# Decay exponents with their mask in one product per head, and large tiles that begin at multiples of 128 bytes

## The reference

```python
acs = jnp.cumsum(dt_k * a_g, axis=1)
seg = acs[:, :, None] - acs[:, None, :]
lmat = jnp.exp(jnp.where(causal, seg, -jnp.inf))
cb = jnp.einsum("blgn,bsgn->blsg", c_k, b_k)
w = cb[..., None] * lmat * dt_k[:, None]
y = jnp.einsum("blsgh,bsghp->blghp", w, x_k)
```

## Time and profile before

| | us |
|---|---|
| median of 3 runs | 1204.3 |
| their lowest and highest | 1203.85 and 1208.6 |
| the profiled execution | 1204.32 |
| its span | 1202.5 |

### The profile page before, as it was taken

One profiled execution on the slowest core, in us unless ns is written; L12 is line 12 of the kernel. 1 busy time (PEld: TensorE's weight loads), 2 busy tenths in 40 slices (PEclk: granted clock), 3 DMA queues, 4 the chain that ended last, 5 costly groups with the idle time before them and its releaser, 6 DMA issues.

```text
span 1202.5 us, 23183 instructions
## 1 busy us (share of the span) xinstructions
PE 1176.9 (98%) x9852; PEld 1076.7 (90%) x9852; DVE 847.2 (70%) x1299; ACT 651.3 (54%) x1171; POOL 151.4 (13%) x143
## 2 busy tenths in 40 slices
PE   8999999999999999999999999999999999999998
PEld 8897789999889898978999988999989878999986
DVE  6677777888557988886788874857577776655542
ACT  4657556666446665644666653665435534644431
POOL 1320000000002332101000000103443311000000
PEclk9999999999999999999999999999999999999999
DMA  8842225565625443353755564442222322755540
GB/s 308 268 141 89 98 101 207 192 210 194 231 106 176 151 182 141 114 184 105 259 196 181 206 245 158 178 176 106 107 107 71 120 93 92 277 196 190 184 167 35
DMA packets 31622, 196.67 MB, mean 164 GB/s; under 512 B 4000, under 2 KB 5664, under 8 KB 9376
## 3 DMA queue, kind: packets, MB, share of 16 engines
q1 hardware_dynamic: 27504, 185.17, 43.1%
q10 hardware_dynamic: 4016, 10.03, 2.6%
HBM read 193.09 MB, written 1.05 MB: 161 GB/s over the span
## 4 chain that ended last, share of the span: by engine, by line
PE 88%; DVE 5%; ACT 3%; issue 2%; POOL 1%; DMA 0%; DVEq 0%; POOLq 0%; ACTq 0%
PE bank L538 24%; PE bank L540 24%; PE bank L539 24%; DVE wlo L527 2%; PE bank L1894 1%; PE bank L1132 1%; PE bank L1189 1%; PE bank L1216 1%; ACT whi L519 1%; PE bank L725 1%; PE bank L2538 1%; PE bank L3005 1%; PE bank L2481 1%; POOL rr L667 0%; PE bank L2525 0%
## 5 line engine op out<-in xcount | busy, mean ns | idle before, releaser
L527 DVE TENSOR_TENSOR wlo<-raw,whi 128x1024 fp32r<-128x1024 f32 x322 | 389.0, 1245 | 87.9 <-ACT whi L519 87.3
L538 PE MATMUL bank<-xT,wlo 128*128 128x256 f32 x1488 | 418.6, 281 | 4.2 <-DVE wlo L527 2.1
L539 PE MATMUL bank<-xT,whi 128*128 128x256 f32 x1488 | 413.1, 278 | 0.0
L540 PE MATMUL bank<-xT,whi 128*128 128x256 f32 x1488 | 413.1, 278 | 0.0
L519 ACT ACTIVATE whi<-raw 128x1024 fp32r<-128x1024 f32 (+1 forms) x349 | 349.2, 1048 | 115.9 <-PE bank L540 86.7
L538 PEld LDWEIGHTS bank<-xT,wlo 128*128 128x128 f32 x1488 | 279.5, 188 | 7.9 <-DVE xc L1601 2.8
L539 PEld LDWEIGHTS bank<-xT,whi 128*128 128x128 f32 x1488 | 279.6, 188 | 0.6 <-issue 0.5
L540 PEld LDWEIGHTS bank<-xT,whi 128*128 128x128 f32 x1488 | 279.4, 188 | 0.0
L667 POOL TENSOR_TENSOR rr<-rr,nhalf 128x1 f32<-128x1 f32 x34 | 24.7, 729 | 710.0 <-DVE rr L655 522.4
L538 PE MATMUL bank<-whi,gT 128*128 128x512 f32 x264 | 104.6, 396 | 0.0
L540 PE MATMUL bank<-whi,gT 128*128 128x512 f32 x264 | 104.4, 395 | 0.0
(11 more groups left out here) (390 smaller groups left out, 1766.5 us busy)
## 6 DMA issues: line engine op xcount, KB each, us to landing
raw<-in_wall SPq DMA_DIRECT2D x173, 1024.0 KB, 4.8
grow<-in_rows ACTq DMA_DIRECT2D x13, 512.0 KB, 5.3
h<-in_x SPq DMA_DIRECT2D x4, 256.0 KB, 5.3
dsk<-in_rows ACTq DMA_DIRECT2D x4, 256.0 KB, 3.4
memx<-in_mem ACTq DMA_DIRECT2D x1, 1024.0 KB, 10.5
out<-h SPq DMA_DIRECT2D x4, 256.0 KB, 2.0
masks<-in_masks SPq DMA_DIRECT2D x1, 580.0 KB, 13.3
D<-Tx ACTq DMA_DIRECT2D x4, 128.0 KB, 5.8
```

Of the source, the lines that this page charges most:

```text
L527: e.tensor_tensor(low, src, high, SUB).then_inc(*up("dve.low", p))
L538: e.matmul(out, a[1], b[0], start=start, stop=False)
L539: e.matmul(out, a[0], b[1], start=False, stop=False)
L540: return e.matmul(out, a[0], b[0], start=False, stop=stop)
```

## The change

It has two parts.

First, a product of four heads becomes four products of 128 columns, one for each head (L1850 after). The moving operand `parts` is 128 rows for each chunk: 96 rows with the three bf16 parts, and 32 rows with a pattern (`fours`) that is one where a column's number divided by 4 is the row's. The stationary operand `pick` holds for each of eight heads 96 rows that select the head and 32 rows (`later`) with -1e30 where a block of four columns lies after the row. So the mask is in blocks of four, and what remains inside a block is done by DVE: `cb` is multiplied by the triangle `tri` first, and `exp` is capped at one in the product with `cb`. ACT makes `pick` once per group (`act_pick`). `segs`, `spread` and the five operations on POOL are gone, and the second subtraction is on 32 rows. The strings of `SSD_ORDER` are written anew for all four engines; they are shown only in part here.

Second, tiles are reordered and padded so that all large ones begin at multiples of 128 bytes.

```diff
+    fours = np.where(r < 32, np.where(c // 4 == r, 1, z), np.where((r >= 96) & (c // 4 > r - 96), n, z))
+    out = [np.where(c > r, n, z), fours, np.where(r % 64 <= np.arange(64)[None, :], z, n)]
-    out.append(((a[:, None] // 4 % 8 == np.arange(8)[None, :]) & (a[:, None] < 96)).astype(np.float32))
-    out.append((a[:, None] % 4 == np.arange(4)[None, :]).astype(np.float32))
+    out.append(((a[:, None] % 32 == np.arange(32)[None, :]) & (a[:, None] < 96)).astype(np.float32))
...
+        h = sb([128, 2, 1024], name="h")
+        xT = [sb([128, 8, 256], f32r, name="xT") for _ in range(2)]
...
+        masks = sb([128, _MASKS + 24], name="masks")
...
+        room = -nc.sbuf_base % 128 // 32
+        if room:
+            sb([128, 8 * room], name="room")
...
-        XW = 16 * 60 + 68
+        XW = 16 * 60 + 96
...
-        segs = sb([96, 2, 4, 128], bf16, sst, "segs")
+        pick = sb([128, 8, 128], bf16, sst, "pick")
...
+        parts = cols[:, _COLS["fc0"][0]:_COLS["fc0"][0] + 128].bitcast(bf16)
+        rest = yy[1][0:64, 0:256]
...
+        def act_pick(e, g):
+
+            e.activation(pick[0:96, :, :], bc(head1[:, 8 * g:8 * g + 8], 128), ACTF.Copy).then_inc(*up("act.scan", "pick", g))
...
+            e.activation(parts[96:128, :].rearrange("p (t n) -> p t n", t=2), fours.unsqueeze(1).to_broadcast([32, 2, 128]),
+                         ACTF.Copy).then_inc(*up("act.ssd", "fours"))
+            e.activation(pick[96:128, :, :], later.unsqueeze(1).to_broadcast([32, 8, 128]), ACTF.Copy).then_inc(
+                *up("act.ssd", "later"))
+            act_pick(e, 0)
             e.wait_ge(*at("pe.proj", C_DT))
...
-            e.tensor_tensor(rest[1], rest[0], part[1], SUB).then_inc(*up("dve.ssd", "rest", 1))
-            e.wait_ge(*at("dve.ssd", "rest", 1))
-            e.tensor_tensor(*spread(rest[1], 0, 2), MUL).then_inc(*up("dve.ssd", "segs"))
...
+            e.tensor_tensor(parts[32:64, :], rest[32:64, :], parts[32:64, :], SUB).then_inc(*up("dve.ssd", "rest", 1))
...
-                e.matmul(bv[:, :].rearrange("p (i n) -> p i n", i=4), identb[:, :],
-                         neg_sl.unsqueeze(1).to_broadcast([128, 4, 128]), start=True, stop=False)
-                e.matmul(bv[:, :], quad[:, q:q + 1].to_broadcast([96, 128]), segs[:, t, :, :].rearrange("p i n -> p (i n)"),
-                         start=False, stop=True).then_inc(*up("pe.scan", "seg", g, t, b2))
...
+                for i in range(4):
+                    r = e.matmul(tl(bv, i), pick[:, 4 * b2 + i, :], tl(parts, t), start=True, stop=True)
+                r.then_inc(*up("pe.scan", "seg", g, t, b2))
...
+                if t and g < 3:
+                    act_pick(e, g + 1)
...
+                e.wait_ge(*at("pe.scan", "cb", g, t))
+                e.tensor_tensor(banks[6][:, 0:128], banks[6][:, 0:128], tri, MUL).then_inc(*up("dve.scan", "cb", g, t))
                 e.wait_ge(*at("act.scan", "seg", g, t, 1))
...
+                e.scalar_tensor_tensor(E[:, :, :], E[:, :, :], 1.0, banks[6][:, 0:128].unsqueeze(1).to_broadcast([128, 8, 128]),
+                                       ALU.min, MUL).then_inc(*up("dve.scan", "w", g, t))
...
             "pe": (
-                "bbbbbbbabbbbbbbabbbbbbbbbbbaabbbbbbababbbbbaaaaabbbaabaabbbbbbaaaabbbbbbaabaabbbbbaabaaabbaaaabbaaaabbbb"
+                "bbbbbbbbabbbbbbabbbbbbbbbbbaabbbbbbbaabbbbbaabaaabbaabaabbbbbbaaaabbbbbbaabaabbbbbaabbaaabaabaabaaaabbbb"
...
-            pool_ssd_parts(e)
```

More of the change, by code:

```diff
@@ L428, in build @@
         ygT = [sb([128, 12, 256], f32r, gd, "yG") for _ in range(2)]
+        kT2, qT2, vT2, zt2 = ([sb([128, 2, 256], st=gd, name="pj") for _ in range(2)] for _ in range(4))
+        ma = ExitStack()
+        qmT = sb([128, 4, 256], st=ma, name="qmT")
+        mP = [sb([128, 512], st=ma, name="mP") for _ in range(2)]
+        mPT = [sb([128, 512], st=ma, name="mPT") for _ in range(2)]
+        ym = sb([128, 2, 512], st=ma, name="ym")
+        mnmx = [sb([128, 4], st=ma, name="mnmx") for _ in range(2)]
+        msum = sb([128, 2, 4], st=ma, name="msum")
+        ma.close()
+        ctx = []
+        for i in range(2):
+            c = {n: sb([128, 4, 128], st=gd, name=n) for n in ("kbg", "kg", "vb")}
+            c["Ct"] = [sb([128, 4, 64], st=gd, name="Ct") for _ in range(2)]
+            c["LY"] = sb([128, 2, 4, 64], st=gd, name="LY")
+            c["TU"] = sb([128, 2, 4, 64], st=gd, name="TU")
+            c["PT"] = sb([128, 4, 64], st=gd, name="PT")
+            c["LT"], c["Ym"] = c["LY"][:, 0, :, :], c["LY"][:, 1, :, :]
+            c["vn"], c["wT"], c["oi"] = c["vb"], by_128(c["LY"]), by_128(c["TU"])
+            c["S"] = c["Ct"][0][:, :, :].rearrange("p a b -> p (a b)").rearrange("p (a b) -> p a b", a=2)
+            ctx.append(c)
+        for c in ctx:
+            c["eqk"], c["rqk"] = (sb([128, 8], st=gd, name="eqk") for _ in range(2))
+            c["brk"], c["kek"], c["sk"], c["ro"] = (sb([128, 4], st=gd, name="sm") for _ in range(4))
         beta = sb([128, 2, 8], st=gd, name="beta")
@@ L437, in build @@
         Ag = sb([128, 8], st=gd, name="Ag")
[L438 to L459, removed]
         DT = xs[:, :].rearrange("p (h t n) -> p h t n", h=8, t=2)
@@ L1706, in act_ssd_first @@
             e.wait_ge(*at("dve.ssd", "rest", 0))
-            e.activation(part[1], rest[0], ACTF.Copy).then_inc(*up("act.ssd", "part", 1))
+            e.activation(parts[0:64, :], rest, ACTF.Copy).then_inc(*up("act.ssd", "part", 1))
         def dve_ssd_first(e, split):
@@ L1728, in dve_ssd_first @@
             e.wait_ge(*at("act.ssd", "part", 0))
-            e.tensor_tensor(rest[0], banks[7][0:96, 0:256], part[0], SUB).then_inc(*up("dve.ssd", "rest", 0))
+            e.tensor_tensor(rest, banks[7][0:64, 0:256], parts[0:64, :], SUB).then_inc(*up("dve.ssd", "rest", 0))
             e.wait_ge(*at("act.ssd", "dec"))
@@ L1847, in pe_seg @@
                 if t == 0:
[L1848 to L1852, removed]
-                e.matmul(bv[:, :].rearrange("p (i n) -> p i n", i=4), identb[:, :],
-                         neg_sl.unsqueeze(1).to_broadcast([128, 4, 128]), start=True, stop=False)
-                e.matmul(bv[:, :], quad[:, q:q + 1].to_broadcast([96, 128]), segs[:, t, :, :].rearrange("p i n -> p (i n)"),
-                         start=False, stop=True).then_inc(*up("pe.scan", "seg", g, t, b2))
+                    e.wait_ge(*at("act.scan", "pick", g))
+                if (g, t) == (0, 0):
+                    e.wait_ge(*at("act.ssd", "later"))
+                    e.wait_ge(*at("act.ssd", "fours"))
+                    e.wait_ge(*at("dve.ssd", "rest", 1))
+                for i in range(4):
+                    r = e.matmul(tl(bv, i), pick[:, 4 * b2 + i, :], tl(parts, t), start=True, stop=True)
+                r.then_inc(*up("pe.scan", "seg", g, t, b2))
                 yield
@@ L1932, in act_ssd_scan @@
                     e.wait_ge(*at("pe.scan", "state", g))
-                    e.wait_ge(*(at("pe.scan", "inter", g - 1) if g else at("pool.ssd", "segs", 1, 2)))
+                    if g:
+                        e.wait_ge(*at("pe.scan", "inter", g - 1))
                     e.activation(stT[:, :], banks[5][:, :], ACTF.Copy).then_inc(*up("act.scan", "state", g))
```

61 lines of the change are left out of this document (18 added, 43 removed).

## The result

The changed kernel takes 1218.5 us (median of 6 runs, 1217.65 to 1220.2), the kernel before 1204.4 in the same comparison (median of 6): ratio 1.0104, interval 1.0086 to 1.0122. It is slower, by 14 us. Forecast was 1200 us, range 1187 to 1219. The profiled execution has a span of 1215.5 us against 1202.5.

The account below looks back on a forecast made before the run. TensorE, busy for 98% of the span, was taken to bound the kernel. Gains of 3.2 us for the products and 1.3 for the waits, with zero for tile starts, took 1204.3 to 1199.8, forecast as 1200 us, range 1187 to 1219.

Parts of the forecast that it names:

- the starts of the tiles: Moving large tiles to multiples of 128 bytes: effect on TensorE's matmul beat taken as zero, the likeliest case.
- Common starts cost: Rival, chance 0.25: `xT` starting at multiples of 128 like the weights slows 256-column products to 120.0 ns; 1218 us.
- starts of tiles are without effect: Reading of the 256-column beats: how a stretch starts sets 113 or 118 ns, not tile starts; likeliest case, 0.40, 1200 us.
- reason for `mT`: The rival's support: `mT` products, the only stretch with both operands at multiples of 128, had the slowest beat, 120.0 ns.
- The rows say nothing changes: 512-column products: start does not matter, as `gT` at a multiple of 128 has 395 ns, `xT` 64 past 396.
- The reading of `P` against `D`: Same DVE line, 701 ns on `P` (64 past) and 688 on `D` (at a multiple): 13 ns, counted as nothing.
- The exponents on TensorE: SSD scan: four bf16 products at 0.24 us replace each of sixteen pairs at 0.44; gain 3.2 us, between 0 and 3.6.
- ScalarE's cover: SSD start: three added activations delay the `xs` copy 1.5 us, but 0.7 us of cover remains, so no cost.
- VectorE's costs: SSD: DVE 3.5 us ahead at 386 us, against eight triangle multiplications costing 2.7 us; 0.8 us ahead overall.
- The waits: SSD: of the 2.8 us TensorE waits for the convolution, 1.3 us were expected to go.

Follow-up runs that it names:

- layout_only: The kernel before with the new places of all tiles and its old scan; 1222.2 us, ratio 1.0134.
- xT_off128: The changed kernel with `xT` moved behind `cols`, 128 bytes past the weights' remainder modulo 256; 1213.9 us.
- before_xs_moved: The kernel before with `xs` alone moved by 128 bytes modulo 256, using unused bytes ahead of and behind it; 1215.7 us, ratio 1.0097.
- xT_off0: The changed kernel with `xT` moved behind `cols` and the small tiles, still at the weights' remainder modulo 256; 1219.5 us, ratio 1.0117.
- before_xT_same: The kernel before with `xT` alone moved to the weights' remainder modulo 256; 1227.6 us, ratio 1.0180.
- xT_off192: The changed kernel with `xT` moved behind `cols`, 192 bytes past the weights' remainder modulo 256; 1193.8 us, ratio 0.9902.
- before_xT_192: The kernel before with 128 unused bytes ahead of `xT`: `xT` 192 past the weights' remainder, `gT`, `yT`, `yG`, `mT` at it; 1201.1 us, ratio 0.9970.

## Why the prediction was wrong

**The step that failed** is the one on the starts of the tiles: "I take zero as the likeliest". The term is +18.3 us (`layout_only`). The rows that speak against it were on the table, and the rival *Common starts cost* has beat (120.0) and time (1218) as measured, and the mechanism but for one thing: what has to be common is the start modulo 256, not modulo 128 (`xT_off128` has `xT` at a multiple of 128 too, and 1213.9 us). What I let decide was that the same `xT` has both 113 and 118, read as "starts of tiles are without effect". In truth both readings hold at once: at distance 64 what runs ahead chooses between two beats (`before_xs_moved`), and at distance 0 there is no such choice (`xT_off0`, `before_xT_same`). That one observation is not set by a tile's start is no evidence against another effect of it. By the Trainium skill (SBUF — State Buffer, Specifications), with its lines of 16 bytes, the places 0 and 64 past a multiple of 128 would be alike and the term zero; the runs have 1227.6 against 1204 us for `xT` alone at the one or the other, and the measurement decides.

**The rival, in its details.** Its reason for `mT` was wrong: `mT` was 128 bytes away from the weights modulo 256, not at their remainder. The 120.0 ns of the earlier trace rows are those of another distance, and for `xT` this distance gave 118.7; why the two differ is open. That its 1218 is the measured time is luck in part: the full sum for 256 columns was 1225, which the faster products of 512 columns bring back to 1218.

**The 512 columns.** "The rows say nothing changes" failed too: they went from 395 to 389 ns. The two rows compared distances 128 and 192 (the weights move, and `xT` at 192 is the stationary one), which are alike there (233.2 and 233.3 ns); distance 0, which the change brings, was in neither. For 512 columns it is the fast one, 226.9 ns, where it is the slow one for 256. It was worth 7 us. The reading of `P` against `D` was wrong as well, without weight: `P` at a multiple of 128 has 700 ns and `D` still 688, so the 13 ns are not the start's.

**The exponents on TensorE: right.** Two groups of four products and seven of eight take the sixteen pairs' place. The timeline of PE around one group of eight:

```profile
435.64 0.28 PE L547 MATMUL bank<-xT,whi 128*128 128x256 f32 x1
435.76 0.62 PE L1850 MATMUL bank<-cols,pick 128*128 128x128 bf16 x8
436.19 0.36 PE L545 MATMUL bank<-xT,wlo 128*128 128x256 f32 x1
436.39 0.28 PE L546 MATMUL bank<-xT,whi 128*128 128x256 f32 x1
```

From 435.64 to 436.39 are 0.75 us; less two steps of 0.12 the eight cost 0.51, so four cost 0.26 (0.29 where four stand alone, at 389.98 us). I took 0.24. The saving is 16 x 0.44 - 2 x 0.29 - 7 x 0.51 = 2.9 us against 3.2. The products follow each other every 55 to 67 ns, 58 on the mean, but for two of the 55 steps, in which TensorE waited. The Trainium skill (TensorE: Matmul & The Clock Gate, Back-to-back issue gap) has about 81 ns for this form; the trace does not agree.

**ScalarE's cover: right.** The copy of the time steps and the matmuls that wait for it, by the timelines of ACT and PE:

```profile
370.72 0.36 ACT L1711 ACTIVATE xs<-bank 96x256 f32<-96x256 f32 x1
...
371.82 0.53 PE L601 MATMUL bank<-masks,xs 96*128 96x32 f32 x4
```

The copy starts 1.1 us ahead of PE's matmuls where it had been 2.6, 1.5 us later as costed, and 0.7 of cover are left.

**VectorE's costs: right.** Its timeline at the SSD's start has the second subtraction at 0.41 us (taken: 0.4) and two pieces of the split at 2.36 (taken: 2.5, where there had been 3.94):

```profile
384.09 0.41 DVE L1751 TENSOR_TENSOR cols<-yy,cols 32x256 bf16<-32x256 f32 x1
384.79 2.36 DVE L534 TENSOR_TENSOR wlo<-raw,whi 128x1024 fp32r<-128x1024 f32 x2 [0.28 <-ACT whi L526]
```

From the first product with `zs` in this stretch to the convolution it takes 8.27 us, from 378.80 to 387.07, where it had taken 11.63, from 374.30 to 385.93: ahead by 3.4 us, costed at 3.5. The triangle costs 0.29 us each time (0.34), and the product with `exp` 1.22 as before.

**The waits: the 1.3 us did not come.** By the waits from 355 to 565 us the convolution's wait is gone from PE, and another is there:

```profile
PE bank L1910 <- DVE yy L1996: 2.0, 1, 2.0
```

PE itself waited 2.1 us for `xc` and 0.4 for this product of the scan before; now 0 and 2.0. The stall went where I had left open that it might ("more than the 2.8 cannot be had and perhaps nothing"), though to VectorE's work in the scan and not to the split. So the scan is worth 2.9 us by the products, and four pairs of kernels that differ in it, and by at most 32 bytes in the places of `identb` and `grow`, have medians 1.3 to 3.7 apart: with the term of waits at nothing the sum fits them.

## What to carry to other kernels

When TensorE is busy for 98% of the time, read its beat from the starts of matmuls, kind by kind, ahead of any change of SBUF's layout, and note each operand's first byte modulo 256 beside it: a lone multiple of 128 bytes says nothing, the distance between the two operands of one product does, and the good one for 256 columns (192 here, with `xT` moving) is not the good one for 512 (0). Since the beat of a long stretch can hang on the place of a tile that it does not read, change one tile at a time, and undo the others' shifts with unused bytes. Here the layout as changed cost 18 us, and one tile's place (`xT_off192`) turned it into 10 us of gain over the kernel before, the scan's share included. A single run can be off by 4 or 8 us when a stretch takes its other beat, so look at the groups in which runs fall, not at the median alone.

## What the runs showed of the hardware

- float32r products, 128 rows and 256 columns, at the full granted clock: with both operands at one remainder modulo 256 bytes they start every 120.0 ns (`xT` in four kernels), 64 or 192 bytes apart every 113.3 or 117.8 in the FFNs, and a stretch of 900 keeps the one it begins with. Products of 512 columns start every 226.9 ns at distance 0 (`gT`) and every 232 to 233 at 128 (`gT`) or 192 (`xT`); at 64 the few with `xT` had 229 (`before_xT_192`, `xT_off192`).
- In the kernel before the beat goes from 117 to 113 ns at four transposes of `xs`; with `xs` 128 bytes further on it stays at 118 behind them, in all three FFNs, which cost 12 us. That the transposes and no other use of `xs` do it is read from the timelines and not tested apart.
- The choice can differ between executions of one program (1195.8, 1200.7 and 1205.2 us in `before_xT_192`; 1203, 1208 and 1212 in the kernel before on one chip).
- The one product on DVE that was compared did not mind: 700 ns and 701 at the two places of `P`.

Why the remainders count was not found. That the load of the next stationary operand and the reading of the moving one get in each other's way at some relative places is a guess that no run tests; whether 192 leans to the fast beat in the FFNs, or the distance of `xs` from `xT` decides, is open too.
